# Memory attention of the retention layer in one stage of 16 tiles, and output weights in another row order

## The reference, cut to what matters

```
def retention_layer(a, mem_k, mem_v, w_in, w_out, gn_g, gn_b, decay):
    proj = a @ w_in
    q, k, v, g, mq = jnp.split(proj, [768, 1536, 2304, 3072], axis=-1)
    ...                                   # rotary q and k, chunkwise retention in both directions, 6 heads of 128
    y = silu(g) * group_norm(y)
    m = memory_attention(mq, mem_k, mem_v)        # 4 heads of 64: softmax(mq k^T / 8) v
    return jnp.concatenate([y, m], axis=-1) @ w_out
```

## Time and profile before

| | |
|---|---|
| Median of the runs (3) | 2518.8 us (2517.79 to 2519.14) |
| Profiled execution | 2516.53 us, of which its span is 2514.5 us |
| TensorE busy | 2362.4 us, 94% of the span |
| DVE, ACT, POOL busy | 48%, 37%, 41% |
| Granted TensorE clock | 0.975 of full on average |
| Chain that ended last | TensorE 84%, ACT 5%, DVE 5%, issue 3%, POOL 3%, DMA 1% |

### The profile page before, as it was taken

The page is one execution under the profiler, slowest core; times in us unless marked ns, Lnnn a source line. Parts: engine busy times, 40 slices in busy tenths (PEclk is TensorE's granted clock), DMA queues, the critical chain, the costliest instruction groups (busy, mean ns, idle before and its releaser), DMA issues.

```text
span 2514.5 us, 30484 instructions
## 1 busy us (share of the span) xinstructions
PE 2362.4 (94%) x11048; PEld 1938.3 (77%) x11048; DVE 1208.7 (48%) x2185; ACT 935.0 (37%) x1821; POOL 1024.5 (41%) x779
## 2 busy tenths in 40 slices
PE   7999998896899999999989999999869999999998
PEld 6788887684788888788867888877747888887886
DVE  5543444435343344476854333343363344345767
ACT  5421222335232333344644444444443333233443
POOL 4122222263777777200342222212637777771001
PEclk9999999997999999999999999999979999999999
DMA  5111112242233233733431111122323333327334
GB/s 205 34 51 59 43 42 84 81 146 92 88 109 113 93 102 116 282 97 95 155 92 42 40 40 40 40 93 93 134 92 109 105 101 99 115 92 293 96 102 146
DMA packets 100481, 254.73 MB, mean 101 GB/s; under 512 B 21599, under 2 KB 21870, under 8 KB 98286
## 3 DMA queue, kind: packets, MB, share of 16 engines
q1 hardware_dynamic: 100334, 252.80, 30.2%
HBM read 188.00 MB, written 64.77 MB: 101 GB/s over the span
## 4 chain that ended last, share of the span: by engine, by line
PE 84%; ACT 5%; DVE 5%; issue 3%; POOL 3%; DMA 1%; SPq 0%; POOLq 0%; ACTq 0%; DVEq 0%
PE PS L1803 24%; PE PS L1805 24%; PE PS L1804 24%; PE PS L2020 3%; PE PS L2250 2%; PE PS L2030 2%; PE PS L2054 1%; PE PS L2127 1%; POOL TW L705 1%; POOL OPS L681 1%; DMA stage<-in_wpack 1%; PE PS L2206 0%; POOL wlo L639 0%; ACT qbd L1193 0%; PE PS L2138 0%
## 5 line engine op out<-in xcount | busy, mean ns | idle before, releaser
L1803 PE MATMUL PS<-AOP,OPS 128*128 128x512 f32 x1232 | 488.4, 396 | 48.3 <-ACT s L928 12.9
L1805 PE MATMUL PS<-AOP,OPS 128*128 128x512 f32 x1232 | 487.0, 395 | 0.0
L1804 PE MATMUL PS<-AOP,OPS 128*128 128x512 f32 x1232 | 487.0, 395 | 0.0
L639 POOL TENSOR_TENSOR wlo<-stage,whi 128x1024 fp32r<-128x1024 f32 x82 | 202.0, 2468 | 539.8 <-ACT whi L841 539.2
L1803 PE MATMUL PS<-aT,whi 128*128 128x512 f32 (+1 forms) x768 | 335.8, 437 | 5.4 <-DVE aT L1281 3.9
L1803 PEld LDWEIGHTS PS<-AOP,OPS 128*128 128x128 f32 x1232 | 235.6, 191 | 103.6 <-issue 42.0
L1805 PE MATMUL PS<-aT,wlo 128*128 128x512 f32 (+1 forms) x768 | 298.5, 389 | 0.0
L1804 PE MATMUL PS<-aT,whi 128*128 128x512 f32 (+1 forms) x768 | 297.9, 388 | 0.0
L918 ACT ACTIVATE OPS<-TW 128x512 fp32r<-128x512 f32 x176 | 110.8, 632 | 451.1 <-POOL TW L705 408.3
L1805 PEld LDWEIGHTS PS<-AOP,OPS 128*128 128x128 f32 x1232 | 235.7, 191 | 50.4
L1804 PEld LDWEIGHTS PS<-AOP,OPS 128*128 128x128 f32 x1232 | 235.8, 191 | 48.9
(11 more groups left out here) (192 smaller groups left out, 3983.9 us busy)
## 6 DMA issues: line engine op xcount, KB each, us to landing
stage<-in_w SPq DMA_DIRECT2D x88, 512.0 KB, 3.6
stage<-in_wpack SPq DMA_DIRECT2D x82, 512.0 KB, 3.6
hidden_scratch<-HT SPq DMA_DIRECT2D x154, 256.0 KB, 2.2
SRAW<-hidden_scratch SPq DMA_DIRECT2D x154, 256.0 KB, 2.7
BW<-in_w SPq DMA_DIRECT2D x16, 1024.0 KB, 11.6
h_scratch<-Hb SPq DMA_DIRECT2D x24, 512.0 KB, 2.7
Hb<-h_scratch SPq DMA_DIRECT2D x24, 512.0 KB, 6.3
cat_scratch<-OC SPq DMA_DIRECT2D x13, 512.0 KB, 3.0
```

What stands on the lines that cost most here:

```text
L639: pool.tensor_tensor(wlo[:, slot, :], stage[:, slot, :], whi[:, slot, :].bitcast(F32), ALU.subtract)\
L1803: pe.matmul(dst, stat[0], mov[0], start=start, stop=False, skip_group_check=onto)
L1804: pe.matmul(dst, stat[0], mov[1], start=False, stop=False, skip_group_check=onto)
L1805: return pe.matmul(dst, stat[1], mov[0], start=False, stop=stop, skip_group_check=onto)
```

## The change: what it does

- RUN_A0 becomes 16 tiles, both pairs of heads, in 19 steps, with the same 32 pieces spread over them; RUN_B0 and everything woven around it goes from the tail stage, on TensorE, DVE and ACT.
- The scores, transposes and products of all 16 tiles use banks 4 to 7.
- The second pair becomes catf[1] by way of OC[1] and cat_scratch; head g becomes catf[g+2], by OC[g % 2]; the last head, catf[7], stays direct. One more tile is stored to DRAM and read back (7 for 6).
- w_out's rows are packed as [6, 7, 0, 1, ..., 5]: the two memory pairs come first in the contraction.
- out_project visits the token tiles of its first unit in the order 0, 1, 3, 2 for 3, 2, 0, 1, with other waits.
- On SP, before_out and two stores stand earlier, between the loads of head 1's units.

```diff
-        RUN_A0 = (0, 8, 0, 0)
-        RUN_B0 = (8, 8, 1, 7)
+        RUN_A0 = (0, 16, 0, 0)
...
-        DIRECT = (6, 7, 15)
+        DIRECT = (7, 15)
...
-            return (r % 2, 2, 3) if RUN_B0[0] <= r < R_END[0] else (4 + r % 2, 6, 7)
+            return 4 + r % 2, 6, 7
...
-                sp.wait_ge(oc_rdy, 8 * l + 8)
+                sp.wait_ge(oc_rdy, 16 if l else 2)
...
+            load_units(U_RETH + 6)
+            store_cat(0)
+            load_units(U_RETH + 7)
+            store_cat(1)
+            before_out(0)
             load_units(U_RETH + 4 + 5)
-            store_cat(0)
             for h in range(1, RH):
                 load_units(U_RETH + 4 * h + 4 + 5)
-                store_cat(h)
+                store_cat(h + 1)
             load_units(U_OUT0 + 5)
-            cat_back(0, range(RH))
-            before_out(0)
+            cat_back(0, range(KD - 1))
...
-                    c = 1 + h
-                    if c >= 2:
-                        act.wait_ge(oc_st[c % 2], stored(c - 2))
+                    c = 2 + h
+                    act.wait_ge(oc_st[c % 2], stored(c - 2))
...
-                    for t in range(9):
-                        mem_step(RUN_B0, t)
                     cat_split(0, range(2))
...
-            for t in range(9, steps(RUN_B0)):
-                mem_step(RUN_B0, t)
...
                 values(h)
-                for t in range(3):
-                    mem_step(RUN_B0, t)
-                scan(h, lambda c: mem_step(RUN_B0, 3 + c // 2) if c in (1, 3, 5) else None)
-                mem_step(RUN_B0, 6)
-                group_norm(h, lambda: mem_step(RUN_B0, 7))
-                mem_step(RUN_B0, 8)
+                scan(h)
+                group_norm(h)
                 cat_split(0, range(2))
                 gated(h)
-                for t in range(9, steps(RUN_B0) + 1):
-                    mem_step(RUN_B0, t)
...
-                            return [[(s_exp, 16)], [(oc_rdy, 8), (pt_ev, 16)], [(oc_rdy, 7)], [(yn_rdy, RH)]][i]
+                            return [[EV[U_OUT0 - 1], EV[U_OUT0 - 2]], [EV[U_OUT0 - 1], EV[U_OUT0 - 2]], [(oc_rdy, 8)], [(yn_rdy, RH)]][i]
...
-                             (3, 2, 0, 1) if l == 0 and th == 0 else range(TT))
+                             (0, 1, 3, 2) if l == 0 and th == 0 else range(TT))
...
             for t in range(steps(RUN_A0)):
+                if t == 8:
+                    pe.wait_ge(*EV[U_RET + 1])
                 mem_step(RUN_A0, t, [(U_RETH + p // KD, p % KD) for p in pieces_at(t, 4 * KD, steps(RUN_A0))])
...
             chunk_scores(RH)
-            for u in range(1, 4):
-                pe.wait_ge(*EV[U_OUT0 - u])
-            for t in range(3):
-                mem_step(RUN_B0, t)
             chunk_states(RH)
-            for t in range(3, 6):
-                mem_step(RUN_B0, t)
             chunk_outputs(RH)
-            for t in range(6, 9):
-                mem_step(RUN_B0, t)
             turn_outputs(RH)
-            for t in range(9, steps(RUN_B0)):
-                mem_step(RUN_B0, t)
             out_project(0)
...
-        tiles(ret[:, 4 * tok:], 2), tiles(ret[:, :4 * tok], 4, RH), rows(a["ret_w_out"][0], [6, 0, 1, 2, 3, 4, 5, 7]),
+        tiles(ret[:, 4 * tok:], 2), tiles(ret[:, :4 * tok], 4, RH), rows(a["ret_w_out"][0], [6, 7, 0, 1, 2, 3, 4, 5]),
```

## The result

The changed kernel takes 2522.83 us in the median of 20 runs (2519.65 to 2528.99), the kernel before 2514.34 in the median of 20 beside them (2509.42 to 2521.34). The ratio is 1.0031, with a 95% interval of 1.0023 to 1.0040: 5.8 to 10 us slower. The forecast was 2524.2, or +5.4. It started from a median of 3 runs, 2518.8, and the kernel before took 4.5 us less beside the changed one; so the two absolute times nearly agree by luck, and what is to be compared is the difference. By the two profiled executions the span grew from 2514.5 to 2520.3, **+5.8 us**.

What follows compares the result with a forecast made beforehand. TensorE, busy 94% of the span, was taken to bound the kernel. Head stage +26.4, tail -22.7 and start of the output projection +1.7 sum to +5.4 us: 2524.2 us on the median, range 2518.5 to 2529.

Steps and rivals of the forecast that it cites:

- Head stage: First scores to last value product: eight more tiles, two waits for DVE's copies and slow clock, +26.4 us.
- the walk of the two queues: Head stage, TensorE and DVE followed step by step: waits of 4.8 and 4.3 us behind the two rotates.
- thin steps: Head stage: 1 + 2 pieces, formerly 3 + 3, between rotate's cause and blocked product; second wait 4.3 us, formerly 2.1.
- The rounds: Five rounds between head and tail stage: text kept, extra store and load of a tile cost nothing, 0 us.
- Tail: Transposes of k to output projection: starts at 451.5 instead of 474.2, with TensorE idle about 14 us, -22.7 us.
- The rival with the low clock throughout: Tail at the low clock throughout, and the k = 2 wait costs clock too: +10 us, 2529; chance 0.12.
- Unit k = 2: Start of output projection: POOL's subtraction waits out DVE's splits, ready at 13.7, asked for at 12.0, +1.7 us.
- Clock at the waits: Head stage: each of the two waits costs its own length plus about 1.9 us of slow clock.
- The rival on the other side: Head stage: rotates don't stop TensorE, so +13.4 there and -7.6 us in all, 2511 us; chance 0.08.

Runs made afterwards that it cites:

- experiment 1: Changed kernel with head 0's q and k left unrotated, plain DVE copies in place of the rotates: 2512.41 us, 0.9989 of the kernel before.
- experiment 2: Changed kernel with the six dexp steps at t = 10 to 15 instead of 4 to 9: 2517.54 us, 1.0008 of the kernel before.
- experiment 5: Changed kernel with all 32 pieces in the first 11 of its 19 steps: 2525.49 us, 1.0039 of the kernel before.
- experiment 4: Changed kernel with 13 extra matmuls, results unused, in the tail's two long waits: 2521.24 us, 1.0023 of the kernel before.
- experiment 9: Kernel before, with only each rotate of head 0 cut in two halves a step apart: 2513.13 us, 0.9984 of the kernel before.
- Experiment 11: As 8, but with the dexp steps at t = 12 to 17 instead of 10 to 15: 2504.77 us, 0.9950 of the kernel before.
- experiment 3: Changed kernel with ACT rounding unit k = 2 of the output projection before its splits: 2521.01 us, 1.0020 of the kernel before.
- experiment 6: Changed kernel with dexp at t = 10 to 15 and head 0's rotates in halves a step apart: 2518.39 us, 1.0003 of the kernel before.
- 7: Changed kernel with unit k = 2 rounded early and the 13 extra tail matmuls: 2517.66 us, 1.0000 of the kernel before.
- 8: Changed kernel with late dexp, halved rotates, early unit k = 2, extra tail matmuls, and rounding beside the rotates two steps later: 2510.47 us, 0.9974 of the kernel before.
- 10: As 8, but without the extra tail matmuls: 2510.28 us, 0.9981 of the kernel before.

## Why the prediction was right, step by step

The mechanism was right, and every stage came within 0.6 us. The difference as a whole came out at +7.8 by ratio for the +5.4 forecast; one term is missing, and it is named below.

- **Head stage, +26.4, measured +26.9.** Waits 4.42 and 4.71 for 4.8 and 4.3, at the products the walk of the two queues named, 27.0 and 56.2 us behind the first scores for 27.3 and 55.4. That rotate is the cause is shown by experiment 1, which takes 12.1 us away; the prediction had 12.9 in waits and clock. That DVE's dexp products ahead of it are a part is shown by 2 (5.0 us), that thin steps are one by 5, for the second wait (4.71 falls to 1.96). Four executions of this stage with the same text took 92.4 to 93.2 us, so the 0.5 us between forecast and measurement lies within their spread.
- **The rounds, 0, measured 0.** The extra store and load, and the moved queue entries, cost nothing there, as forecast.
- **Tail, -22.7, measured -22.65, in part by luck.** The idle times are as walked: POOL's product and the group norm end them. For chunk_states 1.0 us of low clock was put in; its 3.69 is the earlier trace rows's 3.73, so none. For chunk_outputs 1.9 was put in; 8.2 us against the 5.4 of experiment 4 is 2.8. In six other kernels with the same 4.88 us of idle time before them the outputs took 7.0 to 7.7, which is 1.6 to 2.3. Those kernels' tails are 30.5 to 31.1 us, so 32.55 is a long one, and the errors nearly cancel only in this execution. The prediction's addition has a slip too: 434.95 + 5.55 + 1.9 is 442.4 and not 442.6, which would have made it -22.9. The rival with the low clock throughout falls: states ran at full rate.
- **Unit k = 2, +1.7, measured +1.55.** POOL's subtraction began at 487.97, 1.4 us before DVE's splits ended (480.87 to 489.38), and ended 2.2 behind their last; on its own it takes 2.34. So it did nearly nothing until they were done, as the earlier trace rows had it. The Trainium skill, SBUF — State Buffer, section Who interferes with whom, gives the pair of ports whole to the instruction that issues first. In experiment 2 that fits: POOL issued first, and DVE's product sat through it. Here it doesn't decide the matter, since DVE's splits come one behind another and POOL got no turn between them; on a hand-over after one split it would have ended by about 490.9 and not at 491.6.
- **Clock at the waits.** 1.9 us for each of the two in the head; measured, 12.1 (experiment 1) less the 8.3 by which the waits shrank is 3.8, and 2 x 1.9 is 3.8. So close an agreement is luck, for the stage itself varies by 0.8.
- **A term that the forecast lacks: the start of the feed-forward part, +1.1.** The second pair's exponentials no longer stand in the tail, behind ACT's last gate copy. So ACT's function need not change back in the feed-forward part, and a table load of 1.28 us is gone there. ACT rounds the next weights 1.4 us sooner beside DVE's work, and POOL's subtraction begins 1.2 us ahead of a DVE product of two SBUF tiles, where it had begun 0.3 behind it. DVE takes 3.38 us for 2.28, and from one of TensorE's starts behind a wait (608.83, and 614.71 in the changed kernel) to the next it is 8.1 us and not 7.0. First the kernel before, then the changed one:

```profile
606.38 1.28 ACT L933 ACT_TABLE_LOAD   x1
608.60 2.28 DVE L1354 TENSOR_TENSOR RAWA<-RAWB,RAWA 128x2048 f32<-128x2048 f32 x1
608.87 4.43 POOL L681 TENSOR_TENSOR OPS<-stage,OPS 128x512 fp32r<-128x512 f32 x2 [18.21 <-ACT OPS L918]
615.87 0.59 PE L1803 MATMUL PS<-AOP,OPS 128*128 128x512 f32 x1 [2.47 <-DVE AOP L1360]
639.68 0.76 PE L1803 MATMUL PS<-AOP,OPS 128*128 128x512 f32 x1 [6.43 <-ACT s L928]
```

```profile
613.32 5.66 POOL L683 TENSOR_TENSOR OPS<-stage,OPS 128x512 fp32r<-128x512 f32 x2 [16.78 <-ACT OPS L920]
614.48 3.38 DVE L1350 TENSOR_TENSOR RAWA<-RAWB,RAWA 128x2048 f32<-128x2048 f32 x1
622.84 0.77 PE L1794 MATMUL PS<-AOP,OPS 128*128 128x512 f32 x1 [5.12 <-DVE AOP L1356]
646.64 0.77 PE L1794 MATMUL PS<-AOP,OPS 128*128 128x512 f32 x1 [6.10 <-ACT s L930]
```

  DVE's product took 3.36 to 3.38 in all eleven executions with the change, and 2.28 in the two without it (the kernel before and experiment 9). The chain is read from the rows; no experiment moved it alone.
- **The rival on the other side** (rotates stop nothing, -7.6) lacked only its condition. Experiment 1 takes the waits to 0.87 us in all. Its stages then give -7.5, its ratio -2.8 (-5.5 to 0), so the change is slower no more. Experiment 11 does it with the whole computation, and with the edits to the tail, and is faster by 12.

What stays open lies behind that point. The last rows above give the distance between the two kernels where the feed-forward part gets under way: 646.64 - 639.68 = +7.0. For each kernel, this distance to the kernel before, beside what the ratio says (known to 2 to 3 us):

| kernel | at that product | by ratio |
|---|---|---|
| changed | +7.0 | +7.8 |
| 1, 2, 3, 4 | -6.6, +1.7, +3.3, +6.3 | -2.8, +2.0, +5.0, +5.8 |
| 5, 6, 7, 8 | +8.4, -1.8, +1.0, -8.6 | +9.8, +0.8, 0.0, -6.5 |
| 9, 10, 11 | -2.5, -6.1, -12.3 | -4.0, -4.8, -12.6 |

All but experiment 1 agree within that. Behind it single executions drift, though no edit touches what follows: the changed kernel's +7.0 is +4.0 at about 1135 us and +5.8 at the end, and experiment 9's -2.5 becomes -5.0 and -7.3. So that the span's +5.8 equals the sum of the stages is luck, and why experiment 1 stands 3.8 apart stays open. What is said of single terms rests on the stages, and what is said of whole kernels on ratios.

## What to carry to other kernels

Work moved into a stage where the bottleneck engine is full costs its own time, and also thins the cover between a long operation of a helper engine and the product it blocks: walk both queues step by step, and split or move the long operation with the move. A gain in front of a wait on something else is given back there until that wait is removed too (experiments 4 and 7). After such a move re-time the helpers' queues before you judge it: here the same tiles in the same stage give +8 us, or -12 us with the helpers re-timed and the tail mended. Look also at what the helpers no longer do where the work was taken away: one table load less set POOL ahead of DVE some 130 us later.

## What the runs showed of the hardware

- **DVE and POOL can each stop the other.** DVE's product of two SBUF tiles, 0.69 us alone, took 2.76 behind a POOL subtraction of 2.40 that had begun 0.19 before it; one of 2.28 us took 3.38 behind a POOL subtraction that had begun 1.2 before it. POOL's subtraction, 2.34 us alone, took 3.64 begun among DVE's back-to-back splits, and 4.94 in the earlier trace rows.
- **A wait takes clock with it, but not each one.** Behind 4.42 and 4.71 us of idle time in the head the next products ran at the lower of the two levels (2.05 for 1.02), and came back to the full one within a step. With waits of 0.72, 0.71, 0.35 and 1.24 us the whole stage was granted 1.00. A wait of 2.12 us (experiment 6) was followed by scores of 1.02, one of 1.95 in the earlier trace rows by scores of 1.91. Behind the same 3.08 us in the tail, the transposes of k took 1.94 in the earlier trace rows and 1.19 in the changed kernel, and those of v 1.91 there and 1.04 in experiment 3. What decides between the two wasn't found.
- **Products that nothing reads kept the clock up** over waits of 5 and 7 us: outputs 5.4 us for 7.0 to 8.2. From chunk_states to the projection it was 22.2 us in all four kernels with them (4, 7, 8, 11), and 24.5 to 25.7 in the seven others with the change.
- **A change of ACT's function cost 1.28 us each way** (experiment 5, two loads), and within a run of exponentials it stood on TensorE's path.
